# Two-group encoder step on one core: the last MLP's moving rows walked in alternating runs of their halves

## The reference, cut to what matters

```python
def sq_relu_mlp(x, g, w_up, w_down):
    return jnp.square(jax.nn.relu(rmsnorm(x, g) @ w_up)) @ w_down
...
        hp = hp + sq_relu_mlp(hp, norm_mlp[layer], mlp_w_up[layer], mlp_w_down[layer])
        hs = hs + sq_relu_mlp(hs, norm_mlp[layer], mlp_w_up[layer], mlp_w_down[layer])
...
    return (hp[:, N_META:], hs, ...
```

## Time and profile before

| | |
|---|---|
| median of three runs | 2871.09 us |
| profiled execution: span | 2869.05 us |
| TensorE matmuls busy | 2851.2 us (99%), 18666 of them |
| VectorE, ScalarE busy | 50%, 37% |
| DMA | 141 GB/s on average |
| last MLP, its four quarters | 225.39, 224.85, 224.86, 224.69 us |
| granted TensorE clock in these | 1.00 |

### The profile page before, as it was taken

How to read it: one execution, slowest core, us unless ns; L and a number is a source line. 1 busy time by engine, 2 the same in 40 slices (tenths; PEclk the granted TensorE clock), 3 DMA queues, 4 the chain that set the end, 5 groups by cost and what they waited for, 6 DMA issues and landing times.

```text
span 2869.1 us, 45023 instructions
## 1 busy us (share of the span) xinstructions
PE 2851.2 (99%) x18666; PEld 2806.6 (98%) x18666; DVE 1428.7 (50%) x1546; ACT 1070.8 (37%) x1236; POOL 186.4 (6%) x112
## 2 busy tenths in 40 slices
PE   9999999999999999999999999999999999999999
PEld 9997799999999999999999999899999999999999
DVE  7677645543443343344466774546444443444443
ACT  5334533332332233233335633434333333333332
POOL 2000002000000000000221241112000000000000
PEclk9999999999999999999999999999999999999999
DMA  6433024444444444444444444244444444444443
GB/s 232 138 114 110 30 89 140 143 143 140 146 141 141 145 140 141 145 140 141 145 148 155 152 148 148 95 162 147 149 153 147 154 147 152 150 149 153 147 152 136
DMA packets 112783, 405.25 MB, mean 141 GB/s; under 512 B 12656, under 2 KB 14752, under 8 KB 112480
## 3 DMA queue, kind: packets, MB, share of 16 engines
q1 hardware_dynamic: 108864, 392.64, 41.1%
q0 software_dynamic: 1616, 6.31, 0.6%
q10 hardware_dynamic: 2128, 3.66, 0.3%
HBM read 396.48 MB, written 6.09 MB: 140 GB/s over the span
## 4 chain that ended last, share of the span: by engine, by line
PE 97%; DVE 2%; ACT 1%; issue 0%; DMA 0%; ACTq 0%; DVEq 0%
PE PS L1411 31%; PE PS L1416 30%; PE PS L1415 30%; PE PS L1490 0%; ACT pr L483 0%; DVE pr L910 0%; DVE w_lo L843 0%; PE PS L1691 0%; DVE rb L1052 0%; PE PS L1488 0%; PE PS L1866 0%; PE PS L1474 0%; ACT w_hi L435 0%; PE PS L1738 0%; PE PS L1737 0%
## 5 line engine op out<-in xcount | busy, mean ns | idle before, releaser
L843 DVE TENSOR_TENSOR w_lo<-stage,w_hi 128x1024 fp32r<-128x1024 f32 x734 | 920.3, 1256 | 1197.0 <-ACT w_hi L435 1196.6
L435 ACT ACTIVATE w_hi<-stage 128x1024 fp32r<-128x1024 f32 x740 | 784.6, 1061 | 1634.3 <-PE PS L1416 1624.9
L1411 PE MATMUL PS<-xh,w_hi 128*128 128x336 f32 (+1 forms) x3264 | 1025.1, 314 | 1.0 <-DVE kk L1087 0.6
L1416 PE MATMUL PS<-xh,w_lo 128*128 128x336 f32 (+1 forms) x3248 | 1017.1, 313 | 0.0
L1415 PE MATMUL PS<-xl,w_hi 128*128 128x336 f32 (+1 forms) x3248 | 1015.6, 313 | 0.0
L1411 PE MATMUL PS<-hh,w_hi 128*128 128x336 f32 (+1 forms) x2032 | 635.7, 313 | 0.0
L1416 PE MATMUL PS<-hh,w_lo 128*128 128x336 f32 (+1 forms) x2032 | 635.0, 313 | 0.0
L1415 PE MATMUL PS<-hl,w_hi 128*128 128x336 f32 (+1 forms) x2032 | 634.1, 312 | 0.0
L1411 PEld LDWEIGHTS PS<-xh,w_hi 128*128 128x128 f32 x3264 | 613.1, 188 | 3.5 <-issue 1.1
L1415 PEld LDWEIGHTS PS<-xl,w_hi 128*128 128x128 f32 x3248 | 612.5, 189 | 0.4
L1416 PEld LDWEIGHTS PS<-xh,w_lo 128*128 128x128 f32 x3248 | 610.0, 188 | 0.0
(11 more groups left out here) (343 smaller groups left out, 1529.1 us busy)
## 6 DMA issues: line engine op xcount, KB each, us to landing
stage<-in_wstream SPq DMA_DIRECT2D x740, 512.0 KB, 3.3
out_s<-so POOLq DMA_DIRECT2D x8, 256.0 KB, 2.8
x<-in_x_in SPq DMA_DIRECT2D x6, 336.0 KB, 7.1
out_y<-x ACTq DMA_DIRECT2D x3, 672.0 KB, 3.9
dmask<-in_ret POOLq DMA_DIRECT2D x4, 352.0 KB, 5.7
stage<-in_wstream SPq DMA_DIRECT2D x4, 256.0 KB, 3.7
s<-in_s_in POOLq DMA_DIRECT2D x1, 1024.0 KB, 6.2
x<-in_x_in SPq DMA_DIRECT2D x4, 168.0 KB, 3.9
```

What stands on the lines that cost most here:

```text
L435: act.activation(w_hi[:, s, :], stage[:, s, :], ACT.Copy).then_inc(hi_ready, 1)
L843: dve.tensor_tensor(w_lo[:, s, :], stage[:, s, :], w_hi[:, s, :].bitcast(F32), ALU.subtract).then_inc(lo_ready, 1)
L1411: pe.matmul(out, wh, rh, start=first, stop=False)
L1416: mm = pe.matmul(out, wl, rh, start=False, stop=last)
```

## The change

`product` gets a run length. With one, the moving row and the output are read and written in another order: the 320 columns are taken as two halves of 160, and the walk takes `run` columns of the first half, `run` of the second, the next `run` of the first, and so on. Moving row and output have the same order, so each column's result lands where it did. For `run` = 4 there are 80 runs in a row (16 bytes each, the next one 640 bytes further or 624 back), for `run` = 16 there are 20 (64 bytes each). The first three quarters of the last MLP use 4 in the up products and 16 in the down products; the last quarter and all other products stay as they were. No instruction is added, removed or moved.

```diff
+            def woven(cols, run):
+                return cols.rearrange("p (h i e) -> p i h e", h=2, e=run)
+
-            def product(u, j, kt, rh, rl, first, last, bank0, m=4, cols=ALL):
+            def product(u, j, kt, rh, rl, first, last, bank0, m=4, cols=ALL, run=None):
                 s = u % NR
+                if run:
+                    rh, rl = woven(rh, run), woven(rl, run)
                 for o in range(m):
                     ...
                     out = PS[:, bank0 + o, cols]
+                    if run:
+                        out = woven(out, run)
                     pe.matmul(out, wh, rh, start=first, stop=False)
...
-            def chunk(u0, g, xh, xl, i=None, su=0, sg=0, need=None, hook=None, cs=ALL, ks=range(CU)):
+            def chunk(u0, g, xh, xl, i=None, su=0, sg=0, need=None, hook=None, cs=ALL, ks=range(CU), run=None):
...
-                                     4 * (g % 2), cols=cs)
+                                     4 * (g % 2), cols=cs, run=run)
...
-                              hook=sum_squares(n) if whole and c == 0 else None, cs=COLS[n])
+                              hook=sum_squares(n) if whole and c == 0 else None, cs=COLS[n],
+                              run=4 if n == 3 else None)
                     for c in range(4):
                         chunk(u_mlp + 32 + CU * c, g_mlp + 4 + c, hh, hl, f, 64, 8, cs=COLS[n],
+                              run=16 if n == 3 else None,
```

## The result

The changed kernel takes 2899.15 us (2897.56 to 2900.19, four runs) against 2870.2 us before: 1.0098 times as long, 95% interval 1.0087 to 1.0110. It is slower by 29 us, 1%, where I had forecast no change as the likeliest; the time lies in the stated range, on the side of the first rival.

The account below looks back on a forecast made before the run. TensorE's matmuls were taken as the bound. With nothing for either walk, the three quarters stay at 675.1 us and the profiled execution at 2869.05; plus 2.04 us to the median gives 2871.1 us. Range 2825 to 2985 us.

Parts of the forecast that it names:

- Rival 1: Where one run ends and the next begins, in row or output: each break costs time, 103 us more, 2974 us; chance 0.36.
- What bounds the kernel: TensorE's matmuls fill 2851.2 of 2869.1 us; it waits for nobody in the changed quarters, so every ns shows 4608 times.
- The 13 ns of excess: Last MLP's matmuls: 146.39 ns between starts against 133.3 for 320 columns, 13.06 ns over, read as feeding of the moving row.
- Nothing for both walks: Last MLP's first three quarters: runs of 4 and of 16 both cost 0 ns per matmul, 2871 us; chance 0.36.
- The row that I called the nearest: Layer 0's MLP: row addresses differ by 3.3 ns a matmul, 15 us in either direction over 4608 matmuls.
- The sign that I had named for being wrong: Two halves of a quarter differ by more than 1 us while the fourth quarter stays.
- a lost column slot per break: Each break loses 0.457 ns: 36.1 ns in up, 8.7 in down, 103 us more; 0.15 for around this price.
- Rival 2: Successive reads of the moving row clash less when alternating 640 bytes apart: up to 60.2 us less, 2811 us; chance 0.28.

## Why the prediction was wrong, point by point

- **What bounds the kernel.** Right: TensorE alone, so that every ns per matmul showed 4608 times, and no cover took any of it.
- **The 13 ns of excess come from feeding the moving row.** Right, and now shown: it grows with the row's columns, it stays but for 1.1 ns with weights that touch one place, and another order of reading removes 10.55 of the 13.06 ns. What is left of 135.83 over 133.33 is 2.5. The Trainium skill ("TensorE: Matmul & The Clock Gate", Back-to-back issue gap) gives just that, columns / 2.4 + 2.5 ns, for the gap of an isolated matmul at full clock; this case's single-column walk agrees (135.83 and 142.5 ns), and its plain fp32r walk does not (146.39 and 154.44).
- **Nothing for both walks.** This is the step that failed: "I take nothing for both". The prices were 6.95 ns for runs of 4 and 5.28 ns for runs of 16, 16.0 and 12.2 us. I rested it on whole 16-byte pieces being read as often as before. That isn't enough, since runs of 4 and 16 keep the pieces whole and lose; nor is it needed, since single columns from two places cut every piece and gain 10.55 ns (of the longer runs, 10 and 14 columns, which cut pieces, cost 19 to 27 ns). The row that I called the nearest, 3.3 ns between row addresses, had the right size within a factor of about two. The sign that I had named for being wrong is there: up and down halves of 117.77 and 116.48 us, 1.29 us apart, and the fourth quarter as it was. That 2899 us lies in the stated range is luck: its part above 2890 us stood for a lost column slot per break, 2974 us, and the price doesn't go by the break.
- **Rival 1, each break costs time.** Right in sign, wrong as a mechanism. It wanted the up half to lose four times what the down half loses; they lost 5.3 and 4.1 us. Three breaks cost 1.0 ns, 19 cost 5.3, 79 cost 7.0, and with 20 parts 79 breaks gain 3.7. The output, where I left open that the price could lie, pays nothing. The Trainium skill ("PSUM — Partial Sum Buffer", Specifications) says that any non-contiguous pattern slows matmuls significantly; for this output, 112.43 us a half plain and in runs of 2 columns, that isn't borne out. "Advanced Engine Details and Errata" (Memory Cachelines) of the Trainium skill says the same, and beside it that every two consecutive elements should be contiguous; with the second the output agrees, as its shortest runs were of two.
- **Rival 2, the order relieves the feeding.** Wrong for the two walks of this change, right for others, and its highest price, 13.06 ns, was near: single columns from two halves gain 10.55 ns, runs of 4 over 4 or 20 parts 3.4 and 3.7.
- **What stays open.** Why runs of 4, 8 and 16 from two halves cost 5 to 8 ns while 4 or 20 parts by 4 gain, and why 14 parts of 336 columns cost 52 ns. A clash by distance modulo 256 bytes, by the number of parts and by the number of breaks were each tried and fell. Addresses do enter: the starts of the matmuls show that the rows of a half aren't alike. In the plain walk of layer 0's MLP rows kt = 0 to 3 take 153.9, 153.1, 154.6 and 156.2 ns a matmul, and every four rows after them the same again, in each chunk; four rows are 5376 bytes, 21 times 256. With runs of 16 it is 151.1, 151.2, 151.2 and 153.1, with single columns from two places 135.8 for all. A half's price is thus a mean over places that differ, and which addresses clash was not worked out. What in the reading of the row keeps exactly two places at full pace was not tried further.

## What to carry to other kernels

When the engine that sets the time is busy from end to end, first compare its distance of starts with columns per clock: an excess that grows with the row points to the reading of the moving operand, and the order of that reading is then worth measuring: here it lost 1% or gained 5% with no instruction added. Price a new access pattern for operand and output apart, in one kernel with a different walk in each stretch; the stretches add up to whole kernels within 1 us. Don't take "as many bytes, as many pieces" for "as much time" on a path that already runs at its limit.

## What the runs showed of the hardware that I had not expected

- An fp32r row read one column at a time from two places in turn streams at 135.83 ns per 320 columns; the same row in plain order takes 146.39. With four places it is 170.4 ns, with eight 273.3. Why is open.
- An output in PSUM written in runs of 2 to 80 columns from two halves costs nothing, 112.43 us a half as plain, and VectorE reads PSUM with a step of 4 at the plain 1492 ns.
- Where matmuls were 64 or 128 columns long the granted clock fell to 0.51 and 0.50, that is to 1.2 GHz, and so it did (0.50) where single columns were walked over 28 parts of 336 columns, though TensorE counts as busy through all three halves. Before the two falls it was as busy at 1.00, in matmuls of 320 columns and in single columns over 14 parts. The two short ones, then the one with 28 parts:

```profile
2117.29:2278.20 160.91, 160.91 (x772) 160.52 (x771) 59.52 (x44) 43.79 (x43) 8.87 (x4) 0.51 0.33 107
2278.20:2442.08 163.88, 163.88 (x769) 163.88 (x770) 46.28 (x37) 36.37 (x34) 0.00 (x0) 0.50 0.31 104
...
1347.73:1655.02 307.29, 307.29 (x769) 248.49 (x768) 46.60 (x37) 36.51 (x34) 0.00 (x0) 0.50 0.17 55
```
